# Two hybrid layers and a third on one core: a later low part of the input sums, another timetable of quarter products, and a shorter lead for the weight tiles that are made by adding

## The reference, cut to what matters

```python
def swiglu(h, w_gate_up, w_down):
    a, b = jnp.split(h @ w_gate_up, 2, axis=-1)
    return (jax.nn.silu(a) * b) @ w_down

def hybrid_layer(x, ...):
    x = x + 0.5 * swiglu(rms_norm(x, ffn1_norm), ffn1_w_gate_up, ffn1_w_down)
    ...
    x = x + merged @ w_out
    x = x + 0.5 * swiglu(rms_norm(x, ffn2_norm), ffn2_w_gate_up, ffn2_w_down)
    return x
```

## Time and profile before

| | |
|---|---|
| median of 3 runs | 1427.65 us (1426.95 to 1429.47) |
| profiled execution, its own time | 1427.81 us |
| its span | 1426.0 us |
| TensorE (PE) busy | 1414.3 us, 99% |
| VectorE (DVE) busy | 1063.6 us, 75% |
| ScalarE (ACT) busy | 838.7 us, 59% |
| chain that ended last | PE 92%, DVE 5%, ACT 1%, DMA 1% |
| granted TensorE clock | full in all slices but the start |

### The profile page before, as it was taken

One profiled execution on the slowest core, in us unless ns is written; L12 is line 12 of the kernel. 1 busy time (PEld: TensorE's weight loads), 2 busy tenths in 40 slices (PEclk: granted clock), 3 DMA queues, 4 the chain that ended last, 5 costly groups with the idle time before them and its releaser, 6 DMA issues.

```text
span 1426.0 us, 20401 instructions
## 1 busy us (share of the span) xinstructions
PE 1414.3 (99%) x7776; PEld 1207.5 (85%) x7776; DVE 1063.6 (75%) x1638; ACT 838.7 (59%) x1397; POOL 200.9 (14%) x275
## 2 busy tenths in 40 slices
PE   9999999999999999999999999999999999999999
PEld 7888888898888888888888898888888899888887
DVE  7777776676867778786776678777776867778776
ACT  6556556755665556664566746655557765455553
POOL 0121023000001000210050000141048300100000
PEclk9999999999999999999999999999999999999999
DMA  9979665456887768967564466969646335456551
GB/s 376 310 215 241 202 214 180 134 192 226 264 233 182 213 235 271 251 171 213 192 236 148 163 216 184 306 188 244 198 160 222 134 121 192 161 166 219 194 189 59
DMA packets 80592, 292.90 MB, mean 205 GB/s; under 512 B 8944, under 2 KB 9072, under 8 KB 80368
## 3 DMA queue, kind: packets, MB, share of 16 engines
q1 hardware_dynamic: 70992, 257.26, 51.5%
q0 software_dynamic: 9216, 33.56, 13.0%
q10 hardware_dynamic: 288, 0.79, 0.1%
HBM read 290.52 MB, written 1.05 MB: 204 GB/s over the span
## 4 chain that ended last, share of the span: by engine, by line
PE 92%; DVE 5%; ACT 1%; DMA 1%; issue 0%; SPq 0%; DVEq 0%; ACTq 0%
PE bank L716 19%; PE bank L723 10%; PE bank L670 8%; PE bank L671 8%; PE bank L672 8%; PE bank L737 4%; PE bank L742 4%; PE bank L738 4%; PE bank L875 3%; PE bank L879 3%; PE bank L876 3%; PE bank L700 3%; PE bank L707 3%; PE bank L701 3%; DVE wlo L1936 2%; PE bank L969 1%
## 5 line engine op out<-in xcount | busy, mean ns | idle before, releaser
L1936 DVE TENSOR_TENSOR wlo<-raw,whi 128x1024 fp32r<-128x1024 f32 (+1 forms) x433 | 523.4, 1235 | 12.7 <-ACT whi L1332 12.7
L1332 ACT ACTIVATE whi<-raw 128x1024 fp32r<-128x1024 f32 (+1 forms) x433 | 443.0, 1049 | 6.0 <-DMA raw<-w_dram 2.9
L716 PE MATMUL bank<-hx,whi 128*128 128x512 f32 x1344 | 330.8, 393 | 2.1 <-issue 2.1
L716 PEld LDWEIGHTS bank<-hx,whi 128*128 128x128 f32 x1344 | 247.6, 188 | 54.7 <-issue 6.3
L670 PE MATMUL bank<-whi,hid 128*128 128x512 f32 x536 | 211.8, 395 | 0.0
L671 PE MATMUL bank<-wlo,hid 128*128 128x512 f32 x536 | 209.6, 391 | 0.0
L672 PE MATMUL bank<-whi,hid 128*128 128x512 f32 x536 | 208.8, 390 | 0.0
L723 PEld LDWEIGHTS bank<-hx,wlo 128*128 128x128 f32 x1344 | 176.0, 191 | 13.4 <-DVE wlo L1936 4.5
L723 PE MATMUL bank<-hx,wlo 128*128 128x256 f32 x1344 | 179.5, 283 | 3.7 <-DVE wlo L1936 3.7
L1361 ACT ACTIVATE hid<-prod 128x256 fp32r<-128x256 f32 x94 | 39.3, 418 | 161.0 <-DVE prod L2084 75.9
L672 PEld LDWEIGHTS bank<-whi,hid 128*128 128x128 f32 x536 | 100.6, 188 | 21.7
(11 more groups left out here) (300 smaller groups left out, 2188.2 us busy)
## 6 DMA issues: line engine op xcount, KB each, us to landing
raw<-w_dram SPq DMA_DIRECT2D x438, 512.0 KB, 4.4
gates<-w_dram POOLq DMA_DIRECT2D x32, 512.0 KB, 6.7
arena<-w_dram POOLq DMA_DIRECT2D x32, 512.0 KB, 7.6
gates<-w_dram SPq DMA_DIRECT2D x16, 512.0 KB, 6.6
arena<-w_dram SPq DMA_DIRECT2D x16, 512.0 KB, 6.5
gain<-g_dram SPq DMA_DIRECT2D x7, 512.0 KB, 3.4
arena<-c_dram SPq DMA_DIRECT2D x2, 768.0 KB, 6.4
cst<-c_dram SPq DMA_DIRECT2D x1, 1056.0 KB, 10.2
```

The lines of the kernel that those rows point to most:

```text
L716: e.matmul(b[:, :], hi_of(j)[:, k * P:k * P + P], hx[:, k * 2 * S:k * 2 * S + 2 * S], start=k == 0, stop=False, skip_group_check=True)
L1332: e.activation(hi_of(t), raw_of(t), ACT.Copy).then_inc(sem["w_hi"], 1)
L1936: e.tensor_tensor(lo_of(t), raw_of(t), hi_of(t).bitcast(F32), ALU.subtract).then_inc(sem["w_lo"], 1)
```

## The change

It has four parts. `input_low` moves from the end of `N3` to the end of `N4`. `ORDER` is rearranged from `6a` to `2b`: 5a directly behind 6a, 4a one block earlier, 3b before `N10`, 1b before `d8`, 7b before `d9`, 2b before `d10`. The function `lead` shortens `ahead`: a tile of the list `late`, which holds the first halves of the added forms (products 7, 6, 5 and 4), isn't split before the engine is three places (ACT) or two places (DVE) ahead of it, and neither is anything behind it in the plan. And ACT waits for `tokm` before it writes `tokV` of a later chunk, which the new order asks for.

```diff
-ORDER = """N2 N3 d0 1a N4 d1 2a N5 d2 3a N6 d3 7a N7 d4 6a N8 d5 5a N9 d6 4a N10 d7 3b d8 T0a 1b d9 T1a 7b d10 2b d11 6b
+ORDER = """N2 N3 d0 1a N4 d1 2a N5 d2 3a N6 d3 7a N7 d4 6a 5a N8 d5 4a N9 d6 3b N10 d7 1b d8 T0a 7b d9 T1a 2b d10 d11 6b
            N15 d12 5b N16 d13 4b N17 d14 d15 T0b d16 T1b d17""".split()
...
+        late = [j for j, t in enumerate(plan) if form_of(t[0])[1] and t[0][7] == "0"]
+
+        def lead(j, n, most):
+            return max([k for k in range(n + 1) if not any(j + most < t <= j + k for t in late)])
...
-                hi_upto(min(j + HI_LEAD.get(plan[j][0], AHEAD), len(plan) - 1))
+                hi_upto(min(j + lead(j, HI_LEAD.get(plan[j][0], AHEAD), 3), len(plan) - 1))
...
                     if n == 3:
+                        if cc:
+                            E.wait_ge("tokm", 3 * cc - 2)
                         e.activation(tokV, b[:, :], ACT.Copy).then_inc(sem["tokv"], 1)
...
-                lo_upto(min(j + LO_LEAD.get(plan[j][0], AHEAD - 1), len(plan) - 1))
+                lo_upto(min(j + lead(j, LO_LEAD.get(plan[j][0], AHEAD - 1), 2), len(plan) - 1))
...
-                        if i == 3:
+                        if i == 4:
                             input_low()
```

## The result

The changed kernel takes 1474.64 us (median of 4 runs, 1472.77 to 1477.59) against 1428.34 (1426.95 to 1429.47): 1.0327 of the time before, interval 1.0305 to 1.0348. It is slower by 46.3 us, where 28.6 were forecast, and 5.6 above the range. The profiled execution is the slowest of the four, 1477.59 us with a span of 1475.8, 49.8 more than before.

A forecast was written before the change was run, and what follows sets the result against it. PE, busy 99% of the span, was taken as the bound. Losses of 9.2 us in each of four gated stages, 36.8, less 8.2 gained, took 1427.8 to 1456 us; likeliest 1440 to 1467, eight in ten 1431 to 1469.

The forecast's parts named there:

- The waits removed: PE's waits at b4 (5.6 us) and at 6b1 and N15 (2.6 us) go: 8.2 us gained.
- The loop: Chunk a, 7a to 6a: low parts, additions, landings, eviction and sum wait in a circle; PE loses 2.8 us a stage at 6a0.
- u: The end of 7a0's low part; 6a0's low part was forecast to end at u + 13.8 us.
- The bank of 6a: b8 gets 6a's bank, so N8 can't start before t + 9.9; loss 5.4 us a stage, 2 already before 5a0.
- t: The end of 6a0's low part, from which the times of 5a0, N8 and 4a0 were counted.
- 7a0 term: PE waits for 7a0's low part, behind the second half's landing: 1.0 us taken as mean of four stages.
- 4a0 and 4b0: 4a0's low part ready at t + 19.2 against t + 19.1 wanted; in chunk b nothing found late.
- The ring of banks: Followed through the new order: b8 gets the bank of 6a, which before went to 5a.
- A: Rival: the gain alone, since low parts of added forms have slack; 8.2 us off, 1419.6 us; chance 12%.
- B: Rival: only DVE's own order costs, if second halves land within 4.2 us; 3.0 us a stage, 1431.6 us; chance 12%.
- C: Rival: the bank isn't what stops N8, only 5a0 is late; 1443 us; counted within the forecast's 64%.
- D: Rival: one further product, 7a in the burst or 4a, 3 us late each stage; 1468 us and above; chance 8%.

The follow-up runs named there:

- low_only: Kernel before with only the low part of the input sums moved from the end of N3 to the end of N4: 1431.65 us, 1.0020.
- lead_lo: Changed kernel with ACT's old lead of 5 and the shorter lead on DVE alone: 1475.97 us, 1.0323.
- all_lead3: Changed kernel with later form load, product 6 added before b8's and d5's low parts, stage M's old bank order, DVE's lead three places, not two: 1426.45 us.
- no_lead: Changed kernel with the old leads, keeping the later input low part and the new timetable: 1454.44 us, 1.0180.
- after_form: Changed kernel with SP's load of chunk b's H form six plan positions later: 1467.95 us, 1.0275.
- ring_fix: Changed kernel with the order of banks at stage M set back to that of the kernel before: 1471.14 us, 1.0291.
- stalls: Kernel before with six added stops of PE in the last stage, waiting for GpSimd clears of growing size: 1442.91 us, measured once.
- low_form: Kernel before with the later input low part and SP's load of chunk b's H form six plan positions later: 1422.59 us, 0.9964.
- no_lead_c6: Changed kernel with the old leads, and DVE adding product 6 before the low parts of b8 and d5: 1440.07 us, 1.0088.

## Why the prediction was right in kind and wrong in size

- **The waits removed** were right: 5.4 for 5.6 at b4, 3.1 for 2.6 at 6b1 and N15. But "7a has slack" did not stand behind the later low part: alone it loses (`low_only`), because of what SP holds back.
- **The loop** was right. In L0f2 u is 419.81 and 6a0's low part ends at 432.77, u + 13.0 for u + 13.8; the landing took 8.6 for 9.4 (421.25, the issue of 7a1's addition, to 429.85). `lead_lo` and `all_lead3` show that DVE's order closes it.
- **The bank of 6a** was right: t + 9.8 for t + 9.9, and N8 0.11 behind it. What was wrong is its tie to `lead`: `no_lead` has the wait too, 3.6 to 3.8 us. It hangs on DVE being late, which the burst or the loop each bring about.
- **Sizing the 7a0 term** failed. 1.0 was taken, 2.6 to 4.8 came. The bounds named the burst and left it at "would lift the 1.0 too", with no price. `after_form` takes it away and finds 1.6 on average. At 6a0 less came than the 2.8 forecast, 0.3 to 2.3: the landing was quicker (8.6 for 9.4 in L0f2), and in L0f1 and L0f2 PE ran 1.7 us of it off at half clock. So the waits in the gated stages are 40.7 for 36.8.
- **4a0 and 4b0**, "just in time" and "nothing late": 0.27 each, 2.2 us.
- **The ring of banks** was followed through the gated stages and not past them. That left out 2.8 us of wait and 2.0 of slower blocks in `M`, a stage in which the change touches no line. `ring_fix` shows it.
- **The clock** is the largest miss, the step that failed: 12.8 us (10.8 in the gated stages, 2.0 in `M`). The forecast's sum prices each stop of PE at its length and has no term for the clock behind it. `stalls` shows a stop that costs 1.75 us more than its length; that all 12.8 come this way is read from the windows, not shown by a run. Some 3 of the 12.8 are no net loss, since PE would else have waited them at 6a0; this is an estimate from the 1.7 us of 7a1 and a7 in each of L0f1 and L0f2 and from the 6a0 row.
- Forecast net of 28.6, plus 3.9 at 7a0 and 6a0 (40.7 less 36.8), 2.2 at 4a0 and 4b0, 2.8 in `M` and 12.8 of clock, less 0.3 more gained than forecast, is 50.0, against 49.8 in the span.
- **Rivals.** A, the gain alone, and B, with second halves that land within 4.2 us, fell: those behind 7a took 8.5 to 9.8. C fell with the bank. D named the right side ("7a in the burst, or 4a", 1468 and above), with the burst as one of its two causes; the rest of the way came from the clock and from `M`, which it does not have.
- **Left open:** why landings behind 7b are 2 us slower in L0f1 of `low_form`, seen in one execution, and which stops of PE are followed by half clock.

## What to carry to other kernels

A lead in places is only as good as what lies between them: ask what the engine does between the landing and the split, since one place moved DVE's work behind an eviction, and with it 21.5 us. When a wait is moved in a DMA queue, price what goes out at its end: it cost 3 us alone and, with the new order's 7, 26 together; when an order is changed, follow shared rings to the end of the program. And a stop of a busy PE is priced with its clock: where several stops are forecast, give the half clock behind them a term and a range of its own, from nothing to 1.7 us or more at each.

## What the runs showed of the hardware

- The granted clock fell to half for 3.4 or 6.8 us at or behind stops, in a kernel that is busy 97% of the time; each of 3.4 us cost about 1.7 where PE was busy throughout. One stood behind two stops of 1.1 and 1.3 us (`no_lead_c6`, L1f1), while single stops of 3.0 us (`stalls`) and 3.2 us (the changed kernel, L0f2) had none behind them.
- An accumulating DMA of POOL took 13.0 us to land where SP had sent eight loads within 3.75 us, the last 1.1 us before it was issued, and 10.4 where the same eight went out over 8.9 us (377.89 to 386.79), the last 2.2 us before.
